# Prompt tiles of a hybrid encoder: decays, key product, first matrix and its transpose made one tile ahead

## What is computed

```python
diff = G[..., :, None] - G[..., None, :]
gam = jnp.where(incl, jnp.exp(jnp.where(incl, diff, 0.0)), 0.0)      # decays
kk = jnp.einsum('nbhtd,nbhsd->nbhts', k, k)                          # key product
A = jnp.eye(cs) + jnp.where(strict, beta[..., :, None] * kk * gam, 0.0)
sol = lax.linalg.triangular_solve(A, rhs, left_side=True, lower=True, unit_diagonal=True)
p_qk = jnp.einsum('nbhtd,nbhsd->nbhts', q, k) * gam                  # query weights
# then, chunk after chunk, with the state S:
u = u_v_c - jnp.einsum('bhtk,bhkv->bhtv', w_c, S)
o = eG_c[..., None] * jnp.einsum('bhtk,bhkv->bhtv', q_c, S) + jnp.einsum('bhts,bhsv->bhtv', p_c, u)
S = jnp.exp(gL_c)[..., None, None] * S + jnp.einsum('bhsk,bhsv->bhkv', k_end_c, u)
```

## Time and profile before

| | us |
|---|---|
| median of 3 runs | 2611.95 (2611.59 to 2615.35) |
| the profiled execution, own time | 2611.51 |
| its span in the profile | 2609.8 |
| TensorE busy | 2564.2 (98%) |
| VectorE busy | 2105.4 (81%) |
| ScalarE busy | 1213.3 (46%) |
| GpSimd busy | 355.2 (14%) |
| TensorE from the first key product to the fifth tile's `token_rows` | 641.70 to 811.42 |

### The profile page before, as it was taken

How to read it: one execution, slowest core, us unless ns; L and a number is a source line. 1 busy time by engine, 2 the same in 40 slices (tenths; PEclk the granted TensorE clock), 3 DMA queues, 4 the chain that set the end, 5 groups by cost and what they waited for, 6 DMA issues and landing times.

```text
span 2609.8 us, 43704 instructions
## 1 busy us (share of the span) xinstructions
PE 2564.2 (98%) x17600; PEld 2533.9 (97%) x17600; DVE 2105.4 (81%) x2614; ACT 1213.3 (46%) x1921; POOL 355.2 (14%) x186
## 2 busy tenths in 40 slices
PE   9999999998999999999999999999999999999998
PEld 9999999998999799999999999999999999999998
DVE  7979786887787889898877998988757788898756
ACT  5535454343444545455445554645311355454445
POOL 2200003332010120000024200000333300000042
PEclk9999999999999999999999999999999999999999
DMA  4223323232114423223323222223322222332231
GB/s 127 82 81 92 87 78 90 61 84 78 53 36 111 130 65 90 82 82 91 88 71 94 71 83 81 82 85 91 88 77 74 61 78 81 90 89 82 84 97 49
DMA packets 420251, 215.13 MB, mean 82 GB/s; under 512 B 19218, under 2 KB 418011, under 8 KB 420048
## 3 DMA queue, kind: packets, MB, share of 16 engines
q1 hardware_dynamic: 406066, 205.36, 27.6%
q10 hardware_dynamic: 13982, 6.96, 1.0%
HBM read 204.58 MB, written 7.68 MB: 81 GB/s over the span
## 4 chain that ended last, share of the span: by engine, by line
PE 56%; DVE 8%; ACT 2%; issue 1%; POOL 0%; DVEq 0%; ACTq 0%
PE ps L1124 13%; PE ps L1126 13%; PE ps L1125 13%; PE ps L1109 5%; PE ps L1110 5%; PE ps L1113 5%; PE ps L1182 1%; PE ps L1184 1%; PE ps L1183 1%; DVE sumsq L2666 1%; DVE ut L2561 1%; DVE x L3389 1%; DVE tau_lo L2630 1%; DVE r L2752 0%; DVE x L3574 0%
## 5 line engine op out<-in xcount | busy, mean ns | idle before, releaser
L1057 POOL TENSOR_TENSOR wlo<-raw,whi 128x1024 fp32r<-128x1024 f32 (+2 forms) x150 | 339.7, 2266 | 2215.9 <-ACT whi L1852 2215.9
L1124 PE MATMUL ps<-tau_hi,whi 128*128 128x320 f32 x1280 | 396.2, 309 | 0.5 <-ACT sq L2090 0.5
L1125 PE MATMUL ps<-tau_lo,whi 128*128 128x320 f32 x1280 | 395.9, 309 | 0.0
L1126 PE MATMUL ps<-tau_hi,wlo 128*128 128x320 f32 x1280 | 395.9, 309 | 0.0
L1863 ACT CAST whi<-raw 128x512 fp32r<-128x512 f32 (+4 forms) x368 | 258.1, 714 | 195.3 <-PE ps L1126 189.3
L1109 PE MATMUL ps<-xh,whi 128*128 128x320 f32 x1040 | 317.0, 313 | 4.2 <-POOL wlo L1057 2.3
L1110 PE MATMUL ps<-xl,whi 128*128 128x320 f32 x1040 | 313.4, 309 | 0.0
L2577 DVE TENSOR_TENSOR wlo<-raw,whi 128x512 fp32r<-128x512 f32 (+4 forms) x368 | 289.4, 801 | 17.3 <-ACT whi L1863 17.1
L1109 PE MATMUL ps<-hh,whi 128*128 128x320 f32 x928 | 282.4, 312 | 4.4 <-DVE hl L3018 2.1
L1110 PE MATMUL ps<-hl,whi 128*128 128x320 f32 x928 | 280.3, 310 | 0.0
L2577 DVE TENSOR_TENSOR wlo<-wsum,whi 128x1536 fp32r<-128x1536 f32 (+2 forms) x112 | 180.8, 1614 | 81.8 <-ACT whi L1863 80.3
(11 more groups left out here) (498 smaller groups left out, 6120.0 us busy)
## 6 DMA issues: line engine op xcount, KB each, us to landing
raw<-in_ffn_w_gu SPq DMA_DIRECT2D x320, 256.0 KB, 3.8
raw<-in_ffn_w_d SPq DMA_DIRECT2D x96, 192.0 KB, 3.0
raw<-in_w_in_even SPq DMA_DIRECT2D x32, 512.0 KB, 4.1
raw<-in_ffn_w_d SPq DMA_DIRECT2D x32, 384.0 KB, 3.6
raw<-in_w_in_odd SPq DMA_DIRECT2D x24, 512.0 KB, 3.8
raw<-in_ffn_w_gu SPq DMA_DIRECT2D x16, 512.0 KB, 4.3
raw<-in_ffn_w_d SPq DMA_DIRECT2D x64, 128.0 KB, 2.7
raw<-in_w_ple_gate SPq DMA_DIRECT2D x16, 512.0 KB, 4.1
```

The source lines that it names most:

```text
L1057: pool.tensor_tensor(ring(wlo, n), raw[:, slot, 0:kt, :], ring(whi, n).bitcast(fp32), ALU.subtract).then_inc(lo_ready, 1)
L1124: pe.matmul(out, whi[:, w], hi(i), start=(start and i == 0), stop=False, skip_group_check=True)
L1125: pe.matmul(out, whi[:, w], lo(i), start=False, stop=False, skip_group_check=True)
L1126: last = pe.matmul(out, wlo[:, w], hi(i), start=False, stop=(i == kt - 1), skip_group_check=True)
```

## The change

For t = 0 the head stays where it was. For t = 1 to 3 it is made in the tile before: `keys(t + 1)` stands on TensorE between u and the output products, `decays(t + 1)` on ScalarE behind the copy of u, into the tile V2 instead of W1, and `delta_head(t + 1)` on VectorE behind the reciprocal and ahead of "out", `keep_state` and "up0". The query product, its weights and the transposed keys move from the head into levels 1 and 2. The floor of the mLSTM denominator, which also lives in V2, is loaded and made later. On ScalarE the copy of the last outputs and the tile's first `prep` now stand behind the wait for `o`; for t = 0 that `prep` stands behind `decays(0)`. The 96 filler products are dealt out anew (`Z_MID` between the halves of m1, `Z_U` behind u), and the second instead of the third half of each z block pair uses bank 4, which moves the waits on `z_out`.

```diff
@@ -413,12 +413,14 @@
-        Z_HEAD, Z_KS, Z_RT = 4, 8, 8
-        Z_D = {1: 0, 2: 6, 3: 0, 4: 3, 5: 6, 6: 6}
-        Z_NEXT = {1: 7, 2: 2, 3: 8, 4: 4, 5: 2, 6: 8}
+        Z_HEAD, Z_KS, Z_RT, Z_U = 20, 8, 6, 3
+        Z_MID = {2: 2, 4: 2}
+        Z_D = {1: 3, 2: 2, 3: 0, 4: 3, 5: 6, 6: 7}
+        Z_NEXT = {1: 8, 2: 2, 3: 11, 4: 4, 5: 2, 6: 7}
+        Z_BANK = [5, 4, 5, 5]
...
-        ML_ACT = "gates qin floor vt kin kt den".split()
+        ML_ACT = "gates qin vt kin kt floor den".split()
@@ -1335,15 +1337,23 @@
...
-                        if half % 4 != 2 and half:
-                            pe.wait_ge(z_out, half - (half % 4 == 3))
+                        if half % 4 != 1 and half:
+                            pe.wait_ge(z_out, half - (half % 4 == 2))
...
+            def keys(t):
+                k = qkv[:, HA:2 * HA, tile(t)]
+                pe.wait_ge(core["prod"], t + 1)
+                pe.wait_ge(core["expin"], t + 1)
+                per_head(4, lambda h: k[:, h], lambda h: W(0)[:, h]).then_inc(core["kk"], 1)
@@ -1351,19 +1361,7 @@
                 li, l2 = (LVL - 1) * t, (LVL - 2) * t
                 if t == 0:
                     token_rows(0)
-                pe.wait_ge(core["prod"], t + 1)
-                pe.wait_ge(core["expin"], t + 1)
-                per_head(4, lambda h: k[:, h], lambda h: W(0)[:, h]).then_inc(core["kk"], 1)
-                if t:
-                    mlstm_part(t - 1, "up1")
-                z_fill(s, filled, 24)
-                if t:
-                    pe.wait_ge(core["up"], t)
-                per_head(3, lambda h: k[:, h], lambda h: q[:, h]).then_inc(core["np"], 1)
+                    keys(0)
                 z_fill(s, filled, Z_HEAD)
                 for l in range(1, L):
...
-                        c_l = G_b if l == 1 else W(1)
-                        per_head(g, lambda h: c_l[:, h], lambda h: W(6)[:, h], which=TWO[g]).then_inc(core["m1"], 1)
+                        per_head(g, lambda h: W(1)[:, h], lambda h: W(6)[:, h], which=TWO[g]).then_inc(core["m1"], 1)
+                        if g == 0 and l in Z_MID:
+                            z_fill(s, filled, Z_MID[l])
                     if l == 1:
                         pe.wait_ge(core["xt0"], t + 1)
+                        if t:
...
+                    if l == 2:
                         pe.wait_ge(core["np_read"], t + 1)
...
+                    if l == 1:
+                        if t:
+                            pe.wait_ge(core["up"], t)
+                        per_head(3, lambda h: k[:, h], lambda h: q[:, h]).then_inc(core["np"], 1)
...
-                pe.wait_ge(z_out, 4 * t + 3)
+                pe.wait_ge(z_out, 4 * t + 2)
...
                 token_rows(t + 1)
+                z_fill(s, filled, Z_U)
+                if t < NTILE - 2:
+                    keys(t + 1)
                 pe.wait_ge(core["utok"], t + 1)
...
-                    def decays(t):
+                    def decays(t, out):
                         act.wait_ge(beta_G_loaded, 32 * (t + 1))
                         act.wait_ge(core["expin"], t + 1)
-                        if t:
-                            act.wait_ge(core["o"], t)
                         for h in range(HA):
-                            own(act.activation(W(1)[:, h], G_b[:, h], ACT.Relu, scale=-1.0, bias=gcols[:, h:h + 1]).then_inc(act_own, 1), act_own)
-                        act.activation(W(1), W(1), ACT.Exp, scale=-1.0).then_inc(core["gam"], 1)
+                            own(act.activation(out[:, h], G_b[:, h], ACT.Relu, scale=-1.0, bias=gcols[:, h:h + 1]).then_inc(act_own, 1), act_own)
+                        act.activation(out, out, ACT.Exp, scale=-1.0).then_inc(core["gam"], 1)
+                    def gate_exps(t):
                         if 0 < t < NTILE - 1:
-                            act.copy(qkv[:, 16:16 + HA, (t - 1) * P:t * P], heads(2))
                             act.wait_ge(core["up"], t)
                         act.activation(W(2), G_b[:], ACT.Exp)
...
                     act.wait_ge(out_stored, 4 * 16)
                     load_gates(0)
-                    load_floor(0)
+                    decays(0, V(2))
...
                         li, l2 = (LVL - 1) * t, (LVL - 2) * t
+                        if t:
+                            act.wait_ge(core["o"], t)
+                            act.copy(qkv[:, 16:16 + HA, (t - 1) * P:t * P], heads(2))
                         prep(z0 + [2, 3, 5, 7][t])
-                        decays(t)
-                        z_copy(4 * t)
...
-                            for part in {2: ["gates", "qin"], 3: ["floor", "vt", "kin"], 4: ["kt"], 6: ["den"]}.get(l, []):
+                            if l == 6:
+                                z_copy(4 * t + 2)
+                            for part in {2: ["gates", "qin"], 3: ["vt", "kin"], 4: ["kt"], 5: ["floor"], 6: ["den"]}.get(l, []):
                                 mlstm_part(t, part)
                             if l == 1:
+                                gate_exps(t)
                                 act.wait_ge(core["eg"], t + 1)
                                 load_beta_G(t + 1)
-                                if t:
-                                    act.wait_ge(ml_dve, ml(ML_DVE, t - 1, "out"))
-                                    load_floor(t)
+                            if l == 2:
+                                z_copy(4 * t)
+                            if l == 3:
+                                act.wait_ge(core["np_read"], t + 1)
+                                load_floor(t)
...
                                 prep(z0 + [4, 6, 8][t - 1])
-                        z_copy(4 * t + 2)
                         act.wait_ge(core["rt"], t + 1)
                         act.copy(W(8), heads(4)).then_inc(core["rtok"], 1)
                         act.wait_ge(core["u"], t + 1)
                         act.copy(W(1), heads(3)).then_inc(core["utok"], 1)
+                        if t < NTILE - 2:
+                            decays(t + 1, V(2))
                         z_copy(4 * t + 3)
@@ -2789,16 +2808,22 @@
                 dve.wait_ge(core["gam"], t + 1)
                 dve.wait_ge(core["kk"], t + 1)
-                mul(W(4), heads(4), W(1))
+                mul(W(4), heads(4), V(2))
+                if t:
+                    dve.wait_ge(core["u"], t)
                 mul(W(7), W(4), over_heads(level[:, 0, :]))
                 own(dve.tensor_tensor(W(7), over_heads(ident[:]), W(7), ALU.subtract).then_inc(core["xt0"], 1), core["xt0"])
                 own(dve.transpose(flat(6), flat(7)).then_inc(core["x0"], 1), core["x0"])
-                dve.wait_ge(core["eg"], t + 1)
-                own(dve.tensor_tensor(G_b[:], W(4), over_heads(level[:, 1, :]), ALU.mult).then_inc(core["ctl"], 1), core["ctl"])
+                if t:
+                    dve.wait_ge(core["o"], t)
+                masked(1, (LVL - 1) * t)
+            def query_weights(t):
                 dve.wait_ge(core["np"], t + 1)
-                own(dve.tensor_tensor(W(5), heads(3), W(1), ALU.mult).then_inc(core["np_read"], 1), core["np_read"])
+                own(dve.tensor_tensor(W(5), heads(3), V(2), ALU.mult).then_inc(core["np_read"], 1), core["np_read"])
                 if t:
                     mlstm_part(t - 1, "up1")
                 mul(W(5), W(5), over_heads(incl[:, 0, :]))
...
                 if l == 1:
+                    query_weights(t)
+                if l == 2:
+                    dve.wait_ge(core["eg"], t + 1)
...
-                delta_head(t)
+                    delta_head(0)
@@ -2854,14 +2883,16 @@
                 own(dve.tensor_tensor(W(6), v, heads(3), ALU.subtract).then_inc(core["rT"], 1), core["rT"])
                 if t < NTILE - 2:
                     beta_products(t + 1)
+                mlstm_part(t, "floor")
+                if t < NTILE - 2:
+                    gate_columns(t + 1)
                 mlstm_part(t, "scale")
                 if t < NTILE - 2:
-                    gate_columns(t + 1)
+                    delta_head(t + 1)
                 mlstm_part(t, "out")
-                mlstm_part(t, "up0")
                 if t < NTILE - 2:
                     keep_state(t, W(2)[:, :, P - 1])
+                mlstm_part(t, "up0")
...
-                elif part == "scale":
+                elif part == "floor":
                     dve.wait_ge(ml_act, ml(ML_ACT, t, "den"))
                     o1(dve.tensor_tensor(V(7), V(7), V(2), ALU.max))
+                elif part == "scale":
                     o1(dve.reciprocal(V(7), V(7)))
```

More of the change, by code:

```diff
@@ L1337, in z_fill @@
                             pe.wait_ge(lo_ready, n + 1)
-                        if half % 4 != 2 and half:
-                            pe.wait_ge(z_out, half - (half % 4 == 3))
+                        if half % 4 != 1 and half:
+                            pe.wait_ge(z_out, half - (half % 4 == 2))
                     w = [ring(whi, n), ring(whi, n), ring(wlo, n)][m % 3]
```

(16 more changed lines are left out.)

## The result

The changed kernel takes 2618.35 us (median of 20 runs, 2614.39 to 2624.93) against 2611.85 for the kernel before (20 runs beside them, 2608.90 to 2615.36): 1.0027 times as long, with a 95% interval of 1.0021 to 1.0033. It is slower by 0.27%, a little more than the 0.2% that the prediction took for the least that can be told from no change. The profiled execution took 2617.1 us with a span of 2615.4, which is 5.6 more than the span before.

The account below looks back on a forecast made before the run. VectorE's list sets the pace to level 3's last transpose, TensorE from there to the next `token_rows`. 0.7 (first tile) + 4.5 (periods) + 1.3 (clock) = 6.5 on 2611.51, median 0.44 above: 2618.5 us, range 2610 to 2622.5.

Parts of the forecast that it names:

- The hold: Tiles 2 to 4: GpSimd's subtraction works until T + 8.5, so VectorE's level-1 mask ends at T + 9.2, 1.6 late.
- the waits that go: TensorE's five waits a prompt tile, at levels 2 and 4 and the outputs, some 2.5 us a tile.
- T + 6.1: T is the start of a tile's `token_rows`; VectorE's subtraction from the identity ends 6.1 us later, releasing GpSimd.
- the wait for the copy of u: TensorE's wait ahead of the output products: gone in three tiles, left in the last prompt tile, nothing won there.
- The periods: From one `token_rows` to the next: 44.3 instead of 42.8 us, three times, +4.5 in all.
- the list's end: VectorE's operations up to level 3's last transpose end at T + 25.1 instead of T + 23.6, +1.5.
- The first tile: GpSimd holds VectorE's subtraction from the identity; level 3 ends at 664.1 instead of 663.4, +0.7 us.
- The clock: TensorE's granted clock falls behind the first tile's wait ahead of m1: +1.3 us, between 0 and 2.5.
- GpSimd doesn't hold the masks: Rival: mask ends at T + 7.6, period -0.1, first tile 1.6 earlier; -2, 2610, no measurable change; chance 0.14.
- the new filler covers TensorE's waits: Rival: new filler fills every wait, 2.5 us in each of four tiles, -10, 2602; chance 0.11.
- The named weakest step: Where GpSimd starts: a start under the reciprocal, ending by T + 4, would cost nothing.

Follow-up runs that it names:

- experiment 1: Changed kernel with the casts of the second to fourth prompt tile put between ScalarE's two copies at the end of the tile before: 2614.0 us.
- experiment 4: Kernel before, with only the cast of the second to fourth prompt tile put late, behind gam: 2620.25 us.
- experiment 6: Changed kernel with GpSimd's subtraction cut into two halves of the columns: 2612.8 us.
- experiment 7: Changed kernel executed twice more, 2616.39 and 2618.77 us; changed kernel with only the first tile's cast moved to that tile's end, three times more, 2616.43, 2618.84, 2613.48 us.
- experiment 3: Changed kernel with the casts of all four prompt tiles moved, the first to its tile's end, the others into the tile before: 2609.95 us.
- Experiment 5: Kernel of experiment 3 with two VectorE products (query weights' mask, decay of q) moved from behind levels 1 and 2 to behind level 5: 2606.62 us.

## Why the prediction was right

**The hold.** It forecast that GpSimd's subtraction would stand on the masks, in the place of the waits that go. Rows of after show it in all four tiles, experiment 1 takes it away and with it 1.49 to 1.52 a period, and experiment 4 puts it into the kernel before and gets 2.04 to 2.09. The two together, with the sizes under experiment 6, leave no room for the reciprocal or TensorE as the cause. The Trainium skill, "SBUF — State Buffer", section "Who interferes with whom", says that of a VectorE instruction with two SBUF inputs and a GpSimd instruction that reads SBUF, the second to issue stands until the first has finished. The trace agrees: 2.19 for the mask against 0.69.

Some steps of the working came out otherwise, without moving the sum. GpSimd was to be held by the subtraction from the identity until T + 6.1. In the second tile its cast ended at T + 6.14 instead of T + 5.9, and it ran its usual 2.38; only in the first tile was it held (2.74). A held operation was to end its whole usual time behind GpSimd; it ends 0.54 behind it where it takes 0.69 alone, and the one of line 2760 in the earlier trace rows 0.68 behind it where it takes 0.83. TensorE waits 1.70 instead of 2.1, because its filler lasts until T + 7.5. And the wait for the copy of u is not in the list for the last prompt tile either, though `token_rows` and the output products stand 0.84 apart there as before: nothing won, as forecast.

**The periods.** Forecast: m1 at T + 9.2, the list's end at T + 25.1, 19.2 from there, 44.3. Measured: T + 9.20, T + 25.09, 19.37, 44.46. The forecast of +4.5 for three periods came out at +4.53. Two small errors cancel in that sum: the third period of before is 43.18, not 42.8, and the leg from the list's end is 0.17 longer than the sum of its filler and its wait.

**The first tile.** Forecast +0.7, measured +0.87, with the subtraction at 2.76 and the last half of level 3 done at 664.02 against the forecast 664.1.

**The clock** is the term that was mis-sized. Forecast: +1.3, between 0 and 2.5. In the profiled execution the clock stayed at 1.00 behind the first tile's wait, and the term is 0; where it falls, the price is 1.6. The step that failed is the one from the wait to the clock: the fall behind a wait of 2.93 us was carried over to a wait of like length, and experiment 7 shows longer waits without a fall and shorter ones with it. The median of the runs stands 1.25 above the profiled execution; how much of that is the first tile and how much the sample tile the runs of this study do not settle, since only profiled executions show it.

**The time.** The sum gave 2618.0 for the profiled execution (6.5 on 2611.51), which took 2617.1: the clock's 1.3 is missing, and the first tile, the periods and what follows them gave 0.4 more than forecast. The median then stands 1.25 above that execution, where 0.44 was added. So the sum of the tiles is earned by its terms, but that the median came within 0.15 of 2618.5 is in part luck.

**The rivals.** That GpSimd doesn't hold the masks (2610) is refuted by the rows above. Its working was near, though: experiment 3, where none of these masks is held, came out at 2609.95, with periods level with those before and a first tile 1.22 shorter, where 1.6 had been worked out. That the new filler covers TensorE's waits (2602) fails by VectorE's list, as argued. The waits at the halves all but vanished from TensorE's view in experiment 3 too (0.6 us in 3, instead of 4.2 in 16), and the period stayed at 42.95, against a mean of 42.94 before, since VectorE needs as long as ever. Only experiment 5, which shortens that list, brings the period down. The named weakest step, where GpSimd starts, was the one that decides: GpSimd starts at T + 6.2 in the changed kernel, and at T in experiment 1, where the change costs the later tiles nothing.

## What to carry to other kernels

When work moves on one engine, follow what it releases on the others: here a cast on an engine with time to spare decided when GpSimd would run, and GpSimd decided which VectorE operation stood still. Put a GpSimd instruction under a long VectorE operation with one input (a reciprocal of 3.35 us is longer than the 2.37 of the subtraction, and neither stood in experiment 1), or, if it can't be moved, cut it in pieces (which left 0.41 of a hold of 1.50). And when filler closes an engine's waits without moving the period, shorten the list of the engine that was waited for.

## Not expected of the hardware

Between two GpSimd instructions issued one behind the other, VectorE's waiting operation goes first (a mask of 1.10 instead of 2.19 us with the subtraction in halves).

In the first tile the clock fell behind the shorter waits (1.93 and 2.23 us) and stayed behind the longer ones (2.73 and 3.07). In the sample tile the granted clock fell to 0.50 in some executions of one program and not in others, in the kernel before as in the changed one, behind a stretch of narrow products (128x16 and 128x32) in which TensorE shows no idle time above 0.4 us. What starts it there was not tried.
